# Query projection in quarters within the attention steps, key strips of one head, and value pages in two column halves

## The reference, cut to what matters

```python
q = rope((h @ w_q[j]).reshape(b, s, N_HEADS, 2, HEAD_DIM), pos)      # 8 heads x 2 x 64
s = einsum('bqhcd,bkhcd->bhcqk', qi, k) * scale                      # causal mask
p = softmax(s);  a = p[:, :, 0] - lam * p[:, :, 1]
o = einsum('bhqk,bkhe->bqhe', a, v)
o = rms_norm(o, subln_g[j]) * (1.0 - lam_init)
mix = o.reshape(b, s, V_DIM) @ w_o[j]
```

## Time and profile before

| | us |
|---|---|
| median of 3 runs | 2131.28 |
| lowest, highest | 2130.87, 2131.6 |
| the profiled execution | 2134.05 |
| its span on the core | 2132.2 |
| mean granted TensorE clock | 0.973 of full speed |

### The profile page before, as it was taken

The page is one execution under the profiler, slowest core; times in us unless marked ns, Lnnn a source line. Parts: engine busy times, 40 slices in busy tenths (PEclk is TensorE's granted clock), DMA queues, the critical chain, the costliest instruction groups (busy, mean ns, idle before and its releaser), DMA issues.

```text
span 2132.2 us, 39532 instructions
## 1 busy us (share of the span) xinstructions
PE 2040.3 (96%) x16168; PEld 1962.0 (92%) x16168; DVE 931.6 (44%) x1117; ACT 677.5 (32%) x1052; POOL 499.9 (23%) x340
## 2 busy tenths in 40 slices
...
GB/s 193 92 96 89 103 96 88 94 164 167 53 91 89 89 91 100 98 95 88 172 119 90 97 89 96 109 83 136 151 168 158 69 91 89 89 92 100 98 95 40
DMA packets 357660, 224.13 MB, mean 105 GB/s; under 512 B 7988, under 2 KB 340149, under 8 KB 357437
## 3 DMA queue, kind: packets, MB, share of 16 engines
...
## 4 chain that ended last, share of the span: by engine, by line
PE 87%; DVE 7%; issue 3%; DMA 1%; ACT 1%; DVEq 0%; POOL 0%; SPq 0%; ACTq 0%; POOLq 0%
PE ps_all L542 83%; DVE conv_b L1266 1%; DVE conv L1266 1%; PE ps_all L652 1%; PE ps_all L628 1%; DVE w_lo L1112 1%; PE ps_all L700 1%; DVE s_dec L1478 1%; DVE kprod L1475 1%; DMA vT<-v_new_out 0%; PE ps_all L641 0%; PE ps_all L553 0%; DMA x<-xT 0%; PE ps_all L662 0%; DVE t_out L1140 0%
## 5 line engine op out<-in xcount | busy, mean ns | idle before, releaser
L822 ACT ACTIVATE w_hi<-raw 128x1024 fp32r<-128x1024 f32 (+1 forms) x295 | 333.4, 1130 | 1218.0 <-PE ps_all L542 1211.5
L542 PE MATMUL ps_all<-xg_hi,w_hi 128*128 128x260 f32 x3456 | 700.1, 284 | 11.5 <-DVE xg_lo L1122 9.2
L542 PE MATMUL ps_all<-xg_hi,w_lo 128*128 128x260 f32 x3456 | 696.9, 283 | 0.0
L542 PE MATMUL ps_all<-xg_lo,w_hi 128*128 128x260 f32 x3456 | 696.0, 283 | 0.0
L542 PEld LDWEIGHTS ps_all<-xg_hi,w_hi 128*128 128x128 f32 x3456 | 534.1, 189 | 14.1 <-issue 11.1
L542 PEld LDWEIGHTS ps_all<-xg_hi,w_lo 128*128 128x128 f32 x3456 | 533.4, 189 | 0.0
L542 PEld LDWEIGHTS ps_all<-xg_lo,w_hi 128*128 128x128 f32 x3456 | 532.1, 188 | 0.0
L1112 DVE TENSOR_TENSOR w_lo<-raw,w_hi 128x1024 fp32r<-128x1024 f32 (+1 forms) x295 | 398.2, 1350 | 259.2 <-ACT w_hi L822 259.1
L542 PE MATMUL ps_all<-h_hi,w_hi 128*128 128x260 f32 x1664 | 341.0, 285 | 8.0 <-DVE h_lo L1333 8.0
L542 PE MATMUL ps_all<-h_hi,w_lo 128*128 128x260 f32 x1664 | 338.9, 283 | 0.0
L542 PE MATMUL ps_all<-h_lo,w_hi 128*128 128x260 f32 x1664 | 338.5, 283 | 0.0
...
## 6 DMA issues: line engine op xcount, KB each, us to landing
...
```

The lines of the kernel that those rows point to most:

```text
L542: mm = nc.tensor.matmul(unit[slot][:, s, :], w[:, c % 2, k * P:(k + 1) * P], m[:, s * HALF:(s + 1) * HALF], start=kk == 0 and i == 0, stop ...
L822: nc.scalar.activation(w_hi[:, c % 2, 0:w], raw[:, c, 0:w], ACT.Copy).then_inc(hi_made, 1)
```

## The change

Only phases "q" and "o" and the attention between them differ.

- **Queries.** Only chunks 0, 1 and 2 of the query projection stand ahead of the steps. Chunks 3 to 7 are cut into quarters (piece: four tiles, one half of 260 columns, 12 matmuls), one in each of the steps 0 to 19 between scores and turn_a, into PSUM bank 5. DVE takes a half out at every odd step (half_query), splits the next weights and multiplies the sine at every step 4k + 1 (the last two up to step 21); ACT rounds weights and issues the four swaps at steps 4, 8, ... 20; POOL's rope of head h + 3 stands ahead of head_power(h). The queries of three heads are kept (q_slots) in place of all eight.
- **Keys of the samples** are taken by head, not by sample. A unit i is head i // 2 and four samples: eight strips of 128 tokens x 128 features (64 KB) from eight pages, eight transfers in place of one of 512 KB. DVE's product and sum have the same 1024 columns as before. Units stand at steps 1 to 6, then every other step up to 24, and 25 (K_AT). Two units fit in k_strips (four pages did, three of them for keys).
- **Queries of the samples** are turned head by head (turn_q at steps 1, 2, 6, 10, 14, 18, 22), copied by ACT, and handed through DRAM by SP: pass_q stores a head's row, waits for the store, waits for the products of the head before, loads it to all partitions. It stands behind both units of the head before on SP. One slot holds qb where there were two.
- **Page numbers** are read once, all 16, ahead of the first unit.
- **Values** are loaded twice 16 x 256 KB, four heads' columns each, and used at steps 22 to 29 and 31 to 34; both passes have two matmuls of 512 columns for a sample. Scores and weights are made for four heads at a time at steps 12 to 15 and 26 to 30.
- **Others.** vT is loaded by POOL right behind kT at the start of the query phase; before, it was issued after the projection. Six of eight chunks of the output weights are issued between the units.

```diff
+BATCH = NS // 2
+Q_FIRST, Q_SLOTS = 3, 3
+AT_STEP = BATCH * NS + 1
...
-    q_dram = nc.dram_tensor("q_dram", (NS, D), F32, kind="Internal").ap()
+    q_dram = nc.dram_tensor("q_dram", (HEADS, NS * P), F32, kind="Internal").ap()
...
+        kT, q_slots, at_n, q_t = over(HH, room, [("kT", [P, KD, T]), ("q_slots", [P, Q_SLOTS, T]), ("at_n", [P, 2, SEQ]),
+                                             ("q_t", [P, 2, P])])
+        vT, pr, qb = over(HL, room, [("vT", [P, SEQ // P, D]), ("pr", [P, 2, 2, SEQ]), ("qb", [P, NS, P])])
+        late = (KF - MIX) // 2 * T * 4
+        k_strips, = over(HH + KF * T * 4 - late, late, [("k_strips", [P, 2, NPG * BATCH, P])])
+        cs_q, kprod = over(HL + KF * T * 4 - late, late, [("cs_q", [P, 2, T]), ("kprod", [P, NPG * BATCH, P])])
+        v_pages, = over(XG, 2 * KD * T * 4, [("v_pages", [P, NS * NPG, SEQ])])
+        w_all, = over(where["w_hi"][0], 4 * KW * P * 4, [("w_all", [P, 4, KW * P])])
+        aT = [w_all[:, :, KD * P + e * P:KD * P + (e + 1) * P] for e in range(2)]
...
+        q_bank = ps_all[:, 5:6, 0:HALF].broadcast_to([P, 2, HALF])
...
-        SCORES_AT = (BATCH * NPG + 4, NS * NPG + 4)
-        TURN_AT = tuple(s + 2 for s in SCORES_AT)
-        V_AT = {17: 0, 19: 1, 21: 2, 23: 3, 25: 4, 27: 5, 29: 6, 31: 7}
+        SCORES_AT = (12, 26)
+        TURN_AT = (14, 29)
+        V_AT = {22: (0, 0), 23: (0, 1), 24: (0, 2), 25: (0, 3), 26: (0, 4), 27: (0, 5), 28: (0, 6), 29: (0, 7),
+                31: (1, 0), 32: (1, 2), 33: (1, 4), 34: (1, 6)}
+        QUERY_TURN = {1: 1, 2: 2, 6: 3, 10: 4, 14: 5, 18: 6, 22: 7}
+        K_AT = {s: i for i, s in enumerate((1, 2, 3, 4, 5, 6, 8, 10, 12, 14, 16, 18, 20, 22, 24, 25))}
...
-            def load_page(i):
-                if i >= len(K_SLOTS):
-                    sp.wait_ge(kprod_done, i - len(K_SLOTS) + 1)
-                s = i % len(K_SLOTS)
-                sp.dma_start(K_SLOTS[s], page_of(i, cache_k)).then_inc(k_page_full[s], 16)
-            def load_q(b):
-                if b >= 2:
-                    sp.wait_ge(kprod_done, NPG * (b - 1))
-                sp.dma_start(qb[:, b % 2, :], q_dram[b:b + 1, :].broadcast_to([P, D])).then_inc(qb_full[b % 2], 16)
+            def load_k(i, page_ids):
+                h, j = divmod(i, 2)
+                if i >= 2:
+                    sp.wait_ge(kprod_done, i - 1)
+                for g in range(NPG):
+                    for b in range(BATCH):
+                        pg = page_ids[NPG * (BATCH * j + b) + g]
+                        strip = cache_k[bass.ds(pg, 1), :, h * P:(h + 1) * P].rearrange("a t f -> (a t) f")
+                        sp.dma_start(k_strips[:, i % 2, BATCH * g + b, :], strip).then_inc(k_full[i % 2], 16)
+            def pass_q(h):
+                sp.wait_ge(q_copied, h + 1)
+                sp.dma_start(q_dram[h].rearrange("(b f) -> b f", b=NS), q_t[0:NS, h % 2, :]).then_inc(q_stored, 16)
+                sp.wait_ge(q_stored, 16 * (h + 1))
+                if h:
+                    sp.wait_ge(kprod_done, 2 * h)
+                sp.dma_start(qb[:, :, :].rearrange("p b f -> p (b f)"), q_dram[h:h + 1, :].broadcast_to([P, NS * P])
+                             ).then_inc(qb_full, 16)
+            def load_v(n, i, page_ids):
+                if n:
+                    sp.wait_ge(v_page_used, i // NPG + 1)
+                strip = cache_v[bass.ds(page_ids[i], 1), :, n * SEQ:(n + 1) * SEQ].rearrange("a t f -> (a t) f")
+                sp.dma_start(v_pages[:, i, :], strip).then_inc(v_page_full[i], 16)
+            def queries(ph):
+                o = ph.next
+                for c in range(4):
+                    load_chunk(ph, 0, c)
+                load_chunk(ph, 1, 0)
+                load_chunk(ph, 1, 1)
+                sp.wait_ge(chunk_used, ph.chunk0)
+                page_ids = [sp.value_load(pages_s[0:1, i:i + 1], min_val=0, max_val=NPOOL - 1) for i in range(NS * NPG)]
+                load_k(0, page_ids)
+                load_k(1, page_ids)
+                load_chunk(ph, 1, 2)
+                load_chunk(ph, 1, 3)
+                for h in range(HEADS):
+                    pass_q(h)
+                    if h == 6:
+                        sp.wait_ge(chunk_used, ph.chunk0 + ph.chunks)
+                        for i in range(NS * NPG):
+                            load_v(0, i, page_ids)
+                    if h + 1 < HEADS:
+                        load_k(2 * h + 2, page_ids)
+                        if h in (0, 2, 3, 4):
+                            load_chunk(o, 0, (0, 2, 3, 4).index(h))
+                        if h in (5, 6):
+                            load_chunk(o, 1, h - 5)
+                        load_k(2 * h + 3, page_ids)
+                for i in range(NS * NPG):
+                    load_v(1, i, page_ids)
+                load_chunk(o, 1, 2)
+                load_chunk(o, 1, 3)
...
+                            mm = nc.tensor.matmul(to[:, s, :] if to else unit[slot][:, s, :], w[:, c % 2, k * P:(k + 1) * P],
...
+            def turn_q(m):
+                pe.wait_ge(q_s_made, m + 1)
+                nc.tensor.transpose(ps_all[0:NS, 4, 3 * P:4 * P], q_s[:, m, :], cst[:, C_ID:C_ID + P]).then_inc(q_turned, 1)
+            def piece(s):
+                ph, (k, i) = KIND["q"][0], divmod(s, 4)
+                m = Q_FIRST + k
+                if i == 0:
+                    pe.wait_ge(drained, Q0 + m)
+                if i == 2:
+                    pe.wait_ge(half_drained, k + 1)
+                half = KD // 2
+                chunk(ph, m // 4, m % 4, tiles=range(i % 2 * half, (i % 2 + 1) * half), halves=(i // 2,), to=q_bank)
...
+                q = KIND["q"][0]
+                chunk(q, 0, 0, {EARLY: lambda: variance(sums, (rstd_made, made))})
+                chunk(q, 0, 1)
                 pe.wait_ge(in_kt, 16)
                 pe.wait_ge(mask_made, 2)
-                scores(0)
-                scores(1)
-                pe.wait_ge(q_copied, 1)
+                chunk(q, 0, 2, {KD - 4: lambda: turn_q(0), KD - 3: lambda: scores(0), KD - 1: lambda: scores(1)}, to=ps_rot)
                 for s in range(STEPS + 4):
                     if s + 2 < STEPS:
                         scores(s + 2)
+                    if s < 4 * (KD - Q_FIRST):
+                        piece(s)
...
+                def next_query(m):
+                    ahead(KIND["q"][0], m // 4, m % 4)
+                    swap(KD + m, Q0 + m)
+                def copy_q(m):
+                    act.wait_ge(q_turned, m + 1)
+                    if m >= 2:
+                        act.wait_ge(q_stored, 16 * (m - 1))
+                    nc.scalar.activation(q_t[0:NS, m % 2, :], ps_all[0:NS, 4, 3 * P:4 * P], ACT.Copy).then_inc(q_copied, 1)
+                next_query(0)
+                next_query(1)
+                copy_q(0)
                 exps(0)
+                next_query(2)
...
+                    m, late = divmod(s - 4, 4)
+                    if late == 0 and 0 <= m < KD - Q_FIRST:
+                        next_query(Q_FIRST + m)
                     if t == 0 and 0 <= h < HEADS:
+                        if h >= HEADS // 2:
+                            act.wait_ge(kprod_done, 2 * HEADS - 1 if h == HEADS // 2 else 2 * HEADS)
...
+                def half_query(m, s):
+                    q, cols = KIND["q"][0], slice(s * HALF, (s + 1) * HALF)
+                    if s == 0:
+                        dve.wait_ge(half_done, m - Q_FIRST + 1)
+                        dve.wait_ge(rope_done, KD + m - 1)
+                    else:
+                        dve.wait_ge(chunk_used, q.chunk0 + m + 1)
+                    nc.vector.scalar_tensor_tensor(t_gate[:, m % 2, cols], ps_all[:, 5, 0:HALF], SCALE, rstd[:, cols],
+                                                   ALU.mult, ALU.mult).then_inc(drained if s else half_drained, 1)
...
+                def strip_scores(i):
+                    h, j = divmod(i, 2)
+                    dve.wait_ge(k_full[i % 2], 16 * NPG * BATCH * (h + 1))
+                    if j == 0:
+                        dve.wait_ge(qb_full, 16 * (h + 1))
+                    q = qb[:, BATCH * j:BATCH * (j + 1), :].unsqueeze(1).broadcast_to([P, NPG, BATCH, P])
+                    strips = k_strips[:, i % 2, :, :].rearrange("p (g b) f -> p g b f", g=NPG)
+                    nc.vector.tensor_tensor(kprod[:, :, :].rearrange("p (g b) f -> p g b f", g=NPG), strips, q, ALU.mult
+                                            ).then_inc(kprod_done, 1)
+                    dve.wait_ge(kprod_done, i + 1)
+                    nc.vector.tensor_reduce(s_dec[:, :, h, BATCH * 2 * j:BATCH * 2 * (j + 1)],
+                                            kprod[:, :, :].rearrange("p (g b) (c d) -> p g (b c) d", g=NPG, c=2), AX.X, ALU.add
+                                            ).then_inc(kred_done, 1)
...
+                    if s in K_AT:
+                        strip_scores(K_AT[s])
+                    k, i = divmod(s, 4)
+                    if i % 2 and k < KD - Q_FIRST:
```

(12 more changed lines are left out.)

329 lines of the change are left out of this document (153 added, 176 removed).

## The result

The changed kernel is slower: 2154.61 us, median of 4 runs (2151.46 to 2155.56), beside 2131.44 (2130.87 to 2132.75) for the kernel before on the same chip; ratio 1.0105, 95% interval 1.0088 to 1.0123. The forecast was 2125.5 with a range of 2109 to 2143, so the sign was wrong and the range missed. The profiled execution took 2155.56 us, its span is 2153.7; before, 2134.05 and 2132.2.

A forecast was written before the change was run, and what follows sets the result against it. It took the steps as DVE's, newly paced by SP's query hand-over: 1501 + 68 + 7 x 10.4 reaches unit 14 at 1641.8, plus 37.7 ends at 1679.5, not 1685.35; so 2131.3 - 5.8 = 2125.5 us, range 2109 to 2143.

The forecast's parts named there:

- start: Before the steps' units: step 0 begins near 1496, and unit 0 can start at 1501 when its query row has landed.
- inner stretches: DVE's work from a head's first unit product to the end of its second, over seven heads: 68 us.
- hand-overs: SP's chain from a head's second product to the next head's first (strips, store, row), nothing overlapping: 10.4 us, seven times.
- after unit 14: From the start of unit 14 at step 24 to the first product of the output projection: 37.7 us.
- The clock at the output projection: In the first output products: the filled hole should keep PE's clock up, a gain of 2.9 us.
- rival B: Short hand-over, 9.1 us or less: 2116, 2105 at 7.5 us, 2097 if fully hidden; chance 0.23.
- part 1: Ahead of the steps: five of eight query chunks leave the front, so step 0 begins about 36 us earlier.
- part 2: In the steps: twenty pieces of 12 matmuls on PE, 1.45 us each, cost nothing at full clock, covered by DVE.
- C: Hand-over on SP slower: issues of 0.61 us, row 4.7, 12.9 us a head; kernel 2145; chance 0.21.
- D: PE's clock stays at 1.2 GHz through the steps, 3 us more five times; kernel 2141; chance 0.13.

The follow-up runs named there:

- The bands: The changed kernel with the two pages of a sample summed in two separate bands of 32 rows of the bank: 2148.62 us, ratio 1.0089.
- the kernel with the summing matrix: Changed kernel with two bands, queries ahead of strips on SP and ACT's high part first, plus one product per head adding the bands: 2123.73 us, ratio 0.9964.
- The edit of ACT's order alone: The changed kernel with ACT writing the high part before rounding the next query's weights and issuing its four swaps: 2152.8 us, ratio 1.0105.
- the queries-ahead kernel: The changed kernel with the next head's sample queries handed over on SP ahead of the eight strips, not behind them: 2140.87 us, ratio 1.0047.

## Why the prediction was wrong, point by point

Against the profiled execution the forecast was 2134.05 - 5.8 = 2128.3, and 2155.56 was measured: 27.3 us too low. They are 5.5 (start), 6.5 (inner stretches), 0.9 (hand-overs) and 14.4 (after unit 14). Of the 14.4, 2.9 are a gain that the sum took for the first output products, which lie behind the mark; up to the mark itself it had 40.6, and 11.5 were missed.

- **After unit 14, forecast 37.7, measured 52.1: the step that failed.** The sum gave the second value pass "its last 1.3 us" past the hole, because it priced a sample and pass at half of the four products before, some 1 us. That the four had gone to two bands by turns, and that the new code sends both of its products to one, stood in the two kernels, and I read only the number of columns. On the chain from unit 14 on, L741 holds 1.83 + 1.83 + 1.85 + 3.55 + 10.42 = 19.5 us, where the chain of the kernel before, from the step in the earlier trace rows on, holds three samples of 1.87 and I added 1.3: that is 12.6 us more than in the sum. The bands took back 7.9 net and 9.1 without their turning products. Of the 1.4 us of clock gain in L662 and L740 nothing came either: the four transposes took 0.60 instead of 1.13, but the turning products 3.39 instead of 2.76. With that 14.0 would be missing up to the mark, so the rest of the stretch was some 2.5 us shorter than the sum; I haven't broken that down.
- **The clock at the output projection.** I took 2.9 us of gain there, since a filled hole should keep the clock up, and nothing came. It stood at 0.50 (0.51 in the earlier trace rows), though the hole was filled; what is left of idle PE right before it are 2.21 us for av and 0.60 for the squares. In the kernel with the summing matrix, whose turning products take 1.97 us, it was 0.67 over the same length; what sets it there was not tested.
- **The inner stretches, forecast 68, measured 74.5.** The first three came near (8.0, 6.6, 8.3; forecast 8.6, 5.9, 8.9). From head 3 on they were 12.6, 15.0, 13.5 and 10.6, 51.6 together, instead of three times 11.5, 1.3 for the samples and 11.1, 46.9. The sum counted DVE's busy time and put its waits inside a head at nothing, though the trace of the kernel before has them, and rival B counted 9 us of such holes. In steps 4 to 19 of the kernel before:

```profile
L1459 DVE SCALAR_TENSOR_TENSOR h_lo<-ps_all,sub_g,h_hi 128x512 fp32r<-128x512 f32 x3 | 2.3, 751 | 3.7 <-ACT h_hi L1066 3.7
```

  In the changed kernel's seven stretches DVE waited 3.6 us for h_hi, 2.2 for the masked scores and 0.9 for PE's quarters, 6.7 in all; the other 5.0 of its 6.0 us for the quarters (L1479) fell into hand-overs. I had named ACT's 3.5 us per head only as a way to be wrong, for the exponentials; the place where it bites is the high part h_hi, one instruction behind it. The edit of ACT's order alone took 2.4 us from these stretches.

  Two sizes were wrong as well and nearly cancel. A weight split took 1.22 us each of six times, not 2.0, which is 4.7 us less. And single instructions of DVE took far longer than before; their group (unit 0 to 14), and one long and one usual case beside what POOL did:

```profile
L1458 DVE SCALAR_TENSOR_TENSOR coef<-coef,neglam,lsum 128x1 f32<-128x1 f32 x23 | 13.7, 596 | 0.8
...
1613.49 0.22 DVE L1458 SCALAR_TENSOR_TENSOR coef<-coef,neglam,lsum 128x1 f32<-128x1 f32 x1
...
1617.74 1.29 POOL L1721 TENSOR_TENSOR q_slots<-t_act,t_out 128x512 f32<-128x512 f32 x1
1617.82 1.23 DVE L1458 SCALAR_TENSOR_TENSOR coef<-coef,neglam,lsum 128x1 f32<-128x1 f32 x1
```

  The same instruction has a mean of 329 ns in the earlier trace rows. Inside the seven stretches such lengthening (of this group, one at_n and one product) comes to some 6 us, of which the 1.88 us a step already held about 1. No run took POOL's work away, so that POOL is the cause is not tested.
- **The hand-overs, forecast 7 x 10.4 = 72.8, measured 73.7.** Eight issues took 3.9 to 4.3 us (5.7 and 5.9 at the first and last hand-over), forecast 4.1; issue of the store to issue of the row 1.6 (2.1 at the last), forecast 2.3 and an issue; the row 3.7 (4.3 and 4.2 at the last two), forecast 3.7. The mechanism is confirmed by the queries-ahead kernel. But the sum was right partly by luck: I had it as a pure chain, with DVE waiting 4 to 7 us seven times, and DVE waited 8.33 and 6.50, then 1.6 to 2.8 four times and once not at all. From the third hand-over on DVE's and PE's own steps fill most of the same 10 us, so taking SP's part away could not give what the chain alone says: 53.9 us stayed, and the heads grew by 6.2.
- **The start, forecast 1496 and 1501, measured 1499.2 and 1506.5.** I gave the wait for the first rotary sum 1.5 us, from swaps that land in 1.9 to 2.1; it was 3.81, for they landed in 4.8 under kT, vT and sixteen strips at a DMA share of 0.89. I had priced the query row "in traffic" and not the swaps. Part of the miss is scatter: in the kernel with two bands, the same code up to there, the third scores came at 1496.93 and unit 0 at 1504.30. DVE came to step 1 late for the same reason, not for want of the row.
- **The earlier start (part 1) and the quarters on PE (part 2) were near.** 33 us against 36; and the quarters, forecast to cost nothing, cost at least 5 us: that went with three quarters of them, at a lower clock.
- **The rivals.** C's time, 2145, was nearest, but its mechanism (issues of 0.61 us) didn't happen: eight issues with their registers took about 0.5 us each. D's neither: the clock was 0.78 in the steps, not 0.5, and DVE waited 6.0 us for L559. The Trainium skill's pricing of a transfer ("DMA: Bandwidth & Descriptors", "Anatomy of one DMA — SWDGE (gpsimd) path") led to an estimate of 5.9 us for a hand-over; the trace shows 9.4 to 12.5. Store and row together, 5.3 us, are near the 5.2 of that estimate; the eight issues, about 4 us, are not near its 0.4.
